# Strassen-style weight sums moved ahead in each quad, a split opening, bias rows made once, zeroing and table scaling moved to GpSimd

## The reference, cut to what matters

```
def layer(x, pos, p, conv_state, past_ckv, past_kpe, prompt):
    xn = rms_norm(x, p['norm'])
    proj = xn @ p['w_in']          # a_u a_v a_z b_cq b_ckv b_kpe b_z c_h c_b c_c c_z gates
    ws_m = p['a_ws'] * jnp.tril(...)                # A: 128-position chunks
    ya = a_u * (ws_m applied to rms_norm(a_v) + a_bias) * silu(a_z)
    ckv_new = rms_norm(b_ckv); kpe_new = rope(rms_norm(b_kpe)); q = mla_queries(b_cq)
    k, v = mla_keys_values(ckv_all, kpe_all)        # B: 16 heads, block-causal
    yb = attend(q, k, v) * silu(b_z)
    yc = c_b * short_conv(c_c * c_h) * silu(c_z)    # C: depthwise, 3 taps
    g = sigmoid(gates)
    h = g[0] * (ya @ w_pa) + g[1] * (yb @ w_pb) + g[2] * (yc @ w_pc)
    return x + h @ p['w_out']
```

## Time and profile before

| | us |
|---|---|
| median of 3 runs | 6791.76 (6788.22 to 6793.39) |
| the profiled execution | 6785.36 |
| its span, slowest core (7) | 6783.6 (other cores 6754.7 to 6770.5) |
| PE busy | 6417.8, 95% of the span |
| DVE busy | 3642.1, 54% |
| ACT busy | 2468.8, 36% |
| POOL busy | 670.5, 10% |

### The profile page before, as it was taken

The page is one execution under the profiler, slowest core; times in us unless marked ns, Lnnn a source line. Parts: engine busy times, 40 slices in busy tenths (PEclk is TensorE's granted clock), DMA queues, the critical chain, the costliest instruction groups (busy, mean ns, idle before and its releaser), DMA issues.

```text
span 6783.6 us, 117138 instructions; the slowest of 8 cores (6754.7 to 6783.6 us)
## 1 busy us (share of the span) xinstructions
PE 6417.8 (95%) x40156; PEld 3774.5 (56%) x40156; DVE 3642.1 (54%) x6406; ACT 2468.8 (36%) x5376; POOL 670.5 (10%) x1008
## 2 busy tenths in 40 slices
PE   3998999999799899999899999999999999999998
PEld 1654788777455488777644445444434444544443
DVE  4665566556566556555644344555465444455545
ACT  2665331112376522111137673211124767321110
POOL 0002300002000310000200001000020000100000
PEclk9999999999899999999999999999999999999999
DMA  5333454446433254444742223444474222354446
GB/s 114 74 76 63 77 86 79 82 80 145 113 69 77 53 95 85 76 81 82 201 107 42 49 44 61 83 78 78 81 162 108 43 46 43 66 81 78 81 78 155
DMA packets 175648, 571.41 MB, mean 84 GB/s; under 512 B 20056, under 2 KB 34392, under 8 KB 175072
## 3 DMA queue, kind: packets, MB, share of 16 engines
q0 software_dynamic: 120784, 426.31, 37.3%
q1 hardware_dynamic: 54288, 137.61, 6.1%
HBM read 929.57 MB, written 60.53 MB: 146 GB/s over the span
## 4 chain that ended last, share of the span: by engine, by line
PE 82%; DVE 7%; issue 5%; DMA 4%; ACT 1%; SPq 1%; POOL 0%; DVEq 0%; ACTq 0%; POOLq 0%
PE ps L485 82%; DVE W L508 2%; DVE ct L508 1%; DMA xr<-x 1%; DVE R L511 1%; SPq L255 1%; DMA o_ckv<-F 1%; DMA y<-xr 1%; DMA cfm<-cfm_d 0%; DMA xr<-xm 0%; ACT F L504 0%; DVE accx L508 0%; DVE ssS L1546 0%; DMA R2f<-x 0%; DMA b<-bias_d 0%
## 5 line engine op out<-in xcount | busy, mean ns | idle before, releaser
L485 PE MATMUL ps<-R,W 128*128 128x512 bf16 (+3 forms) x19296 | 3305.8, 327 | 22.2 <-DVE R L511 7.4
L485 PEld LDWEIGHTS ps<-R,W 128*128 128x128 bf16 x19296 | 1888.1, 98 | 1305.0 <-issue 78.7
L508 DVE TENSOR_TENSOR ct<-ps,ct 128x260 f32<-128x260 f32 (+1 forms) x1500 | 740.9, 511 | 922.1 <-PE ps L485 905.6
L255 POOL DMA_DIRECT2D W<-wst x796 | 425.0, 534 | 5907.4 <-PE ps L485 4865.6
L504 ACT ACTIVATE ct<-ps 128x260 f32<-128x260 f32 (+1 forms) x600 | 269.8, 456 | 1406.6 <-PE ps L485 1347.1
L485 PE MATMUL ps<-xs,W 128*128 128x260 bf16 (+1 forms) x4224 | 644.2, 309 | 59.5 <-DVE ct L508 59.4
L485 PEld LDWEIGHTS ps<-xs,W 128*128 128x128 bf16 x4224 | 399.8, 97 | 303.9 <-issue 122.8
L508 DVE TENSOR_TENSOR W<-W,W 128x1024 bf16<-128x1024 bf16 (+1 forms) x600 | 503.5, 866 | 20.8
L504 ACT ACTIVATE P<-ps 128x512 bf16<-128x512 f32 x768 | 426.3, 599 | 207.6 <-PE ps L485 202.5
L504 ACT ACTIVATE sg<-ct 128x520 bf16<-128x520 f32 (+1 forms) x384 | 242.5, 633 | 695.4 <-DVE ct L508 695.3
L485 PE MATMUL ps<-qpe,kp 128*128 128x512 bf16 (+2 forms) x1280 | 432.8, 349 | 0.0
(11 more groups left out here) (170 smaller groups left out, 6180.5 us busy)
## 6 DMA issues: line engine op xcount, KB each, us to landing
W<-wst POOLq DMA_DIRECT2D x796, 512.0 KB, 5.4
xr<-x SPq DMA_DIRECT2D x16, 520.0 KB, 13.4
xr<-xm SPq DMA_DIRECT2D x16, 520.0 KB, 8.0
y<-xr SPq DMA_DIRECT2D x16, 520.0 KB, 10.4
Vsc<-vcur SPq DMA_DIRECT2D x16, 512.0 KB, 4.1
Ksc<-kcur SPq DMA_DIRECT2D x32, 256.0 KB, 4.6
vpast<-Vsc SPq DMA_DIRECT2D x16, 512.0 KB, 3.9
kpast<-Ksc SPq DMA_DIRECT2D x32, 256.0 KB, 2.6
```

The lines of the kernel that those rows point to most:

```text
L255: self.E[Q].dma_start(out=out, in_=in_, **kw).then_inc(self.sem[name], 16)
L485: S.op('pe', lambda e: e.matmul(out, lhsT=lhsT, rhs=rhs, start=start, stop=stop, skip_group_check=skip), [lhsT, rhs], [out], stop if inc i ...
L508: S.op(eng, lambda e: e.tensor_tensor(out=out, in0=a, in1=b, op=op), [a, b], [out], hold=0.1 + size(a) / (960 if eng == 'dve' else 300), l ...
```

## The change

Four things are done.

1. In `quad`, the three sums for the next quad (`half`, `half`, `diff`) are put in `fq` first and are written to DVE's row right after the copy of the second product, ahead of the `part` that reads the third; before, they stood behind that `part` and ahead of the one that reads the fourth. `Sa` keeps its place behind the third product. Two `fill` calls go.
2. The opening of the program: the first 352 columns of x are loaded first, in four DMAs; the weight loads wait for them; the constants are loaded from ACT's queue. Squares of odd tiles are added on POOL into `accy`, those of even tiles on DVE into `accx`, and the fp32 matmul against ones runs over both.
3. Bias rows of both layers are made once before pass 0, in `biasr[:, l]`; `wsmT` is made on POOL.
4. At the start of each pass the whole of `kp0` and `kp1` is zeroed on POOL, and the three tables are scaled there.

```
-        def w_issue():
+        def w_issue(rk=()):
...
-        w_issue()
         C0 = L.C0
+        for i, a in ((0, L.Rf[1]), (1, L.Rf[2])):
+            for j in (0, 4):
+                S.dma('sp', a[:, j:j + 4, 0:352], xt[0][8 * i + j:8 * i + j + 4, :, 0:352]..., ('xo', i, j), wk=[('open', i, j)])
+        for c0, w in CHS[0][1:]:
+            for i, a in ((0, L.Rf[1]), (1, L.Rf[2])):
+                S.dma('sp', a[:, :, c0:c0 + w], ..., ('xl', i, c0))
...
-            S.dma('sp', t.ap() ..., d, 'c_' + t.name)
+            S.dma('act', t.ap() ..., d, 'c_' + t.name)
+        w_issue([('open', i, j) for i in range(2) for j in (0, 4)])
+        for l in range(2):
+            S.dma('sp', C0['wsr%d' % l][:, :, :], wsT_d[l], 'wsr%d' % l)
+            for r in (0, 32):
+                S.dma('sp', C0['b32'][r:r + 1, l, :], bias_d[l], 'b32%d%d' % (l, r))
...
         def stat(p, x, n, c0, w, eng='dve'):
-            acc = L.PN[p]['accx'][:, c0:c0 + w]
+            two = p == 0 and eng == 'pool'
+            acc = (C0['accy'] if two else L.PN[p]['accx'])[:, c0:c0 + w]
...
-            mm(ps[b][:, 0:w], L.onesf[:, :], L.PN[p]['accx'][:, c0:c0 + w], True, True)
+            if p == 0:
+                mm(ps[b][:, 0:w], L.onesf[:, :], C0['accy'][:, c0:c0 + w], True, False)
+            mm(ps[b][:, 0:w], L.onesf[:, :], L.PN[p]['accx'][:, c0:c0 + w], p != 0, True)
...
-            memset(L.kp[0][64:128, :], 0.0)
-            memset(L.kp[1][0:64, :], 0.0)
+            memset(L.kp[0][:, :], 0.0, 'pool')
+            memset(L.kp[1][:, :], 0.0, 'pool')
...
-            tsm(B['tabK'][:, 0:T], B['tabK'][:, 0:T], L.krc[:, l:l + 1])
+            tsm(B['tabK'][:, 0:T], B['tabK'][:, 0:T], L.krc[:, l:l + 1], 'pool')
...
-                fq.extend([half(0), half(1), diff, both])
+                return [half(0), half(1), diff, both]
...
+                ahead = prep(*nxt_) if nxt_ is not None else []
+                fq.extend(ahead[0:3])
                 a = banks()
...
                 t2 = copy(c)
+                drain()
                 z = banks()
                 prod(z, lambda k: sa[:, k, :], lambda k, s, w: xs[0][:, k, s:s + w], True)
                 part(t1, z, t1, ALU.subtract)
-                if nxt_ is not None:
-                    prep(*nxt_)
-                fill(3)
+                fq.extend(ahead[3:])
+                fill(1)
                 q = banks()
...
                 use(1, 0, t)
-                fill(1)
...
                 use(1, 1, t2)
-                fill(2)
...
-                stat(0, X0(n)[:, c0:c0 + w], n, c0, w)
+                stat(0, X0(n)[:, c0:c0 + w], n, c0, w, 'pool' if n % 2 else 'dve')
...
-                tt(L.wsmT[:, l, g, :], C0['wsr'][:, g, :], C0['tril'][:, :], ALU.mult)
+                tt(L.wsmT[:, l, g, :], C0['wsr%d' % l][:, g, :], C0['tril'][:, :], ALU.mult, 'pool')
+        cp(L.biasr[0:1, :, :], b32[0:1, :, :])
+        cp(L.biasr[32:33, :, :], b32[32:33, :, :])
+        tt(L.biasr[32:33, :, :], b32[32:33, :, :], L.biasr[32:33, :, :], ALU.subtract)
         for p, (ti, l) in enumerate(passes):
-            S.dma('sp', b32[0:1, :], bias_d[l], 'b32a')
-            S.dma('sp', b32[32:33, :], bias_d[l], 'b32b')
-            cp(L.biasr[0:1, :], b32[0:1, :])
-            cp(L.biasr[32:33, :], b32[32:33, :])
-            tt(L.biasr[32:33, :], b32[32:33, :], L.biasr[32:33, :], ALU.subtract)
```

More of the change, by code:

```diff
@@ L345, in allocate @@
                             ('mean64f', [128, 64], F32),
-                            ('ident', [128, 128], BF16), ('wsmT', [128, 2, 4, 128], BF16), ('biasr', [128, 512], BF16), ('cst', [128, 2, 8, 2], BF16),
+                            ('ident', [128, 128], BF16), ('wsmT', [128, 2, 4, 128], BF16), ('biasr', [128, 2, 512], BF16), ('cst', [128, 2, 8, 2], BF16),
                             ('cst32', [128, 8, 2], F32), ('ngc', [128, 2, 16], F32), ('kvgc', [128, 2, 4], F32), ('qgc', [128, 2, 4], F32),
@@ L433, in allocate @@
     L.H = place([Region(L.base[L.yc.name], ya_at + RB // 2), Region(kp_at, kp_at + 8320)], setof('hs', 5, [128, 8, 520], BF16))
-    L.C0 = place([Region(scr, end)], [('iot', [128, 128], F32), ('tril', [128, 128], F32), ('wsr', [128, 4, 128], F32), ('b32', [64, 512], F32)])
+    L.C0 = place([Region(scr, end)], [('iot', [128, 128], F32), ('tril', [128, 128], F32), ('wsr0', [128, 4, 128], F32), ('wsr1', [128, 4, 128], F32), ('b32', [64, 2, 512], F32), ('accy', [128, 1040], F32)])
     return L
@@ L547, in w_issue @@
                     continue
-                S.dma('pool', L.W[s][:, :], wst[l, BIDX[b]], 'W%d' % s)
+                S.dma('pool', L.W[s][:, :], wst[l, BIDX[b]], 'W%d' % s, rk=rk)
         def need(key):
@@ L680, in emit @@
         memset(L.nhalf[:, :], -0.5)
-        memset(L.biasr[:, :], 0.0)
+        memset(L.biasr[:, :, :], 0.0)
         for t, d in ((L.ngc, ngc_d), (L.kvgc, kvg_d), (L.qgc, qg_d), (L.qngc, qng_d), (L.kngc, kng_d), (L.qrc, qrc_d), (L.krc, krc_d), (L.cwc, cwc_d)):
-            S.dma('sp', t.ap() if hasattr(t, 'ap') and callable(t.ap) else t[:], d, 'c_' + t.name)
+            S.dma('act', t.ap() if hasattr(t, 'ap') and callable(t.ap) else t[:], d, 'c_' + t.name)
+        w_issue([('open', i, j) for i in range(2) for j in (0, 4)])
[3 more added lines that the diff above has]
+                S.dma('sp', C0['b32'][r:r + 1, l, :], bias_d[l], 'b32%d%d' % (l, r))
         S.dma('pool', L.scv[:], scv_d, 'c_scv')
@@ L696, in stat @@
         def stat(p, x, n, c0, w, eng='dve'):
-            acc = L.PN[p]['accx'][:, c0:c0 + w]
-            if n < 2 and (p, c0) not in begun:
-                begun.add((p, c0))
+            two = p == 0 and eng == 'pool'
+            acc = (C0['accy'] if two else L.PN[p]['accx'])[:, c0:c0 + w]
+            if n < 2 and (p, c0, two) not in begun:
+                begun.add((p, c0, two))
                 act(acc, x, AF.Square)
@@ L768, in run_pass @@
                 S.dma('sp', L.kp[1][64:128, 0:1024], kpsc[l], 'kp1', rk=[('kp', l)], us=4)
-            tsm(B['tabK'][:, 0:T], B['tabK'][:, 0:T], L.krc[:, l:l + 1])
-            tsm(B['tabC'][:, 0:T], B['tabC'][:, 0:T], L.qrc[:, l, 0:1])
-            tsm(B['tabS'][:, 0:T], B['tabS'][:, 0:T], L.qrc[:, l, 1:2])
+            tsm(B['tabK'][:, 0:T], B['tabK'][:, 0:T], L.krc[:, l:l + 1], 'pool')
+            tsm(B['tabC'][:, 0:T], B['tabC'][:, 0:T], L.qrc[:, l, 0:1], 'pool')
+            tsm(B['tabS'][:, 0:T], B['tabS'][:, 0:T], L.qrc[:, l, 1:2], 'pool')
             def latent(which, gain, dst, out):
@@ L1263, in run_pass @@
             after = {seq[i][0]: (seq[i + 1] if i + 1 < len(seq) else None) for i in range(len(seq))}
-            prep(*seq[0])
+            fq.extend(prep(*seq[0]))
             xs = [L.X['xs%d' % i][:, :, 0:H] for i in range(3)] + [xn[:, 8:16, 0:H], xn[:, 0:8, H:T]]
@@ L1351, in run_pass @@
                     b = G.get()
-                    rb = L.biasr[:, g * 128:(g + 1) * 128].unsqueeze(1).to_broadcast([128, 4, 128])
+                    rb = L.biasr[:, l, g * 128:(g + 1) * 128].unsqueeze(1).to_broadcast([128, 4, 128])
                     mm(ps[b][:, :].rearrange("p (s t) -> p s t", t=128), L.ones[:, :], rb, True, False)
@@ L1361, in run_pass @@
                     b = G.get()
-                    mm(ps[b][:, 0:16], L.ones[:, :], L.biasr[:, g * 128:g * 128 + 16], True, False)
+                    mm(ps[b][:, 0:16], L.ones[:, :], L.biasr[:, l, g * 128:g * 128 + 16], True, False)
                     mm(ps[b][:, 0:16], vn[0:16, 8, c * 128:(c + 1) * 128], L.wsmT[0:16, l, g, 0:16], False, True)
```

6 lines of the change are left out of this document (3 added, 3 removed).

## The result

| | before | after |
|---|---|---|
| runs compared | 6790 us (median of 4) | 6672 and 6669 us |
| ratio, with its 95% interval | | 0.9826 (0.9803 to 0.9850) |
| the profiled execution | 6785.4 | 6671.9 |
| its span, slowest core | 6783.6 (core 7) | 6670.4 (core 5) |
| PE busy, share of the span | 6417.8, 95% | 6405.2, 96% |

The change makes the kernel 1.7% faster, some 118 us by the ratio and 113 us between the profiled executions. Forecast were 134 and a time of 6658. In some executions of any of these kernels the cores of one die show a lower granted clock and take longer; ratios leave such executions out, and where only such a profile exists (experiments 5 and 9) cores of the other die are read.

A forecast was written before the change was run, and what follows sets the result against it. PE, busy 95% of the span, bounds the kernel, so only its waits and granted clock matter. Quads 81, opening 23 + 7, three starts 25, less 2, make 134 us: 6658 us, range 6622 to 6697 (eight in ten: 6622 to 6710).

The forecast's parts named there:

- Weight sums in z and gate quads: Sums moved into DVE's idle hole spare PE's wait before product 6: 0.78 us a narrow quad, 0.16 a wide one.
- rivals A: Only the quads gain; POOL's work shuts DVE out at pass starts and in the opening: gain 73, 6719 us, chance 0.10.
- B: In quads, sums start late through a slot or load, so product 5 waits, not 6: gain 76, 6716 us, chance 0.07.
- C: Slower: late-landing blocks hold DVE, then PE, in 96 gate quads; 6946 us if landings take 17 us; chance 0.03.
- 44 have this shape: Of 50 quads in a narrow pass, 44 (z paths and gates) lose 0.78 us each: 69 us gained over two passes.
- one of the things that I had named as showing the prediction wrong: In the quads, product 5 waiting in place of product 6 would show the prediction wrong; no size given.
- The w_out term (-2): All w_out quads together: 5 us gained in most, 7 lost in the first of each pass, net -2.
- about 2 us later in each of four passes: First w_out quad: mixes and sums, 7.2 us, precede reading product 3, so PE waits in product 5; minus 7 together.
- the gain counted for the other w_out quads (5 us): W_out quads after the first gain like the others, some 9 us, of which half (5 us) was counted.
- The opening: Program start: loading x's first columns first starts PE at about 79.5, not 102.44, gaining 23, plus 7 behind it.
- The split of the adding brings nothing by itself: In the opening, sharing additions of squares between POOL and DVE gains nothing, as one buffer per engine replaces two shared.
- The starts: Starts of passes 1 to 3: DVE loses bias wait, zeroing and scaling; 10, 9 and 9 us, 25 together after contention.

The follow-up runs named there:

- experiments 5: The changed kernel with zeroing and scaling back on DVE, bias rows still made once; pass 1, 2 and 3 starts 5.6, 15.1 and 4.6 us longer than the changed kernel's.
- 9: The changed kernel with the first eight weight loads issued at once, not behind x; no whole time given, projections start at 96.01 us.
- Experiments 3: The changed kernel with waiting DVE jobs put behind the reading of product 4 in each pass's first z and first w_out quad; profiled execution 6620.2 us.
- 4: The changed kernel with late sums in the first z quad and w_out's mixes of h split, mostly made beside the last pb products; ratio 0.9747 to the kernel before.
- experiment 1: The kernel before with only the new order in quad; ratio 0.9905 to the kernel before.

## Why the prediction was right, and where it was not

**Weight sums in z and gate quads: right.** Forecast 0.78 and 0.16 a quad, measured 0.78 and 0.16 in all but a few of 172, 80 us together. The step that made it (the sums fit into DVE's hole, product 5 does not wait in place of 6) is what the trace shows, and rivals A, B and C have nothing for them: no `ct` wait over 0.3 us in passes 2 and 3 between the first z quad and w_out, no load that DVE waits for there.

**"44 have this shape" was wrong by one quad a pass.** I gave every z quad the shape of the earlier trace rows. In the first of each pass DVE comes late from `vn` and has no hole; the sums make PE wait 4.0 instead of 1.4 us. These four quads lost 13.2 us where I had counted a gain of 2, and that is nearly all of what the z and gate quads lack (67 measured from product 3 to product 3, 83 forecast). Experiments 3 and 4 show it: with the sums put late there, the four passes get 19.0 us shorter, more than 4 x 2.6, because the clock falls behind the longer wait. What happened here, product 5 waiting in place of 6, is rival B's mechanism and one of the things that I had named as showing the prediction wrong; it came from DVE's other work and not from a slot or a load, and only in these quads and in w_out.

**The w_out term (-2) was mis-sized: it is -25.6** (-27.6 by the second table). Two steps of it failed. For the first quad the mechanism was in the text: 7.2 us of DVE work ahead of reading product 3, and PE waiting in product 5. The wait came, 7.5 to 7.7 us, 3 more than the 0.81 and 3.72 that pass 2 had in its first quad before; "about 2 us later in each of four passes" is 3.3 to 4.0, 14.5 together instead of 7. The larger miss is the gain counted for the other w_out quads (5 us). The second to fifth lose 13.1 together, all of it in passes 0 to 2, because the sums there meet POOL's additions and take 4.6 instead of 2.6 us, and PE waits in front of product 5; of the earlier trace rows I had made nothing at this place. In both, some 10 us are the clock, which the term left out: it fell to 0.77 behind the first wait of pass 2.

**The opening: right sum (30 forecast, 28.3), with one wrong step.** "The split of the adding brings nothing by itself" should have read: costs 7. I had written down that POOL can add only after the loads (18.5, measured 21.9), but not that DVE alone would be through with all sixteen tiles by then. By the text the first addition on POOL ended at 19.3 and the last at 28.6; the first reduction came at 33.3, and the start was 3 us late, by 82.6 against 79.5. x ahead of the weights is shown to carry 13.4 us. Behind it the wait of 7.41 us is gone, as forecast, but another that I had not counted, of 8.68 us on DVE's `F` at 159.07, is still there with 5.02.

**The starts: 38.7 where 25 was forecast.** The 3 us of contention were right (2.55 in pass 1). Pass 2 gave 19.9 for 9: beside the 3.50 of the earlier trace rows a second wait of 4.3 to 5.5 us on ACT's `F` went, which cores 4 to 7 had and I had not looked for, and with the waits gone the clock stayed up (0.95 in one window of 20 us, 1.00 in the next two); before it was 0.74 from 3420 to 3440 and 0.83 from 3460 to 3480. And 4.4 of the 38.7 are the quads' (experiment 1), not the starts'.

**POOL's work.** Zeroing took 1.8 us for 128 x 2064, at my lower bound, and three scalings 4.3: 7.9 us for the chain taken as 11. In pass 1 DVE added squares at its usual 0.52 us during the zeroings (1722.3 to 1725.9). This is the second half of the rule in the Trainium skill (page "SBUF — State Buffer", section "Who interferes with whom"), of which the trace of before had no row: an operation of GpSimd that only writes does not disturb a two-input operation of DVE. This case now agrees with both halves.

Of the things named as tests, `ct` below 60 us failed (73.4), by the two errors above; product 5 did wait in place of 6 in the quads named above; the `F` waits at the starts are 4.8 in pass 1 (below 3 was asked) and none in passes 2 and 3; the rest came as written. The forecast time was 14 us too low (21 between the profiled executions): errors of -34 (z and w_out, 10 and 24) and +14 (starts) partly cancelled, so that the sum came this near is in part luck.

## What to carry to other kernels

Work for later belongs into the hole in front of what the bounding engine waits for, but only where there is a hole: look at the first and last member of every stage apart, since DVE arrives there from other work. Weigh a wait by its length and not by its share of a sum: 16.8 us more of idle time, gathered in a few long waits, cost 26.8, and 2.5 us off a wait of 4 brought 5. A second engine for an additive job helps only if its queue is free and its work does not stretch that of the first; count when each engine could start before splitting. And when a row that moved is used as a mark in time, take a second mark that did not move.
